# Other PSUM banks for the second FFN chunk, and a new order of the first FFN steps on three engines

## The reference, cut to what matters

```python
h = rmsnorm(x, ffn_norm)
g = jnp.einsum('bsd,df->bsf', h, w_gate)      # 1024 x 2816
u = jnp.einsum('bsd,df->bsf', h, w_up)        # 1024 x 2816
x = x + jnp.einsum('bsf,fd->bsd', jax.nn.silu(g) * u, w_down)   # 2816 x 1024
return rmsnorm(x, final_norm)
```

## Time and profile before

| | |
|---|---|
| median of 3 runs | 301.69 us (301.49, 301.69, 302.96) |
| profiled execution, its own time | 301.57 us |
| its span in the trace | 299.8 us |
| mean granted TensorE clock | 0.982 |
| PE busy | 287.1 us, 96% of the span |
| DVE busy | 265.1 us, 88% |
| ACT busy | 189.7 us, 63% |
| DMA, HBM read | 55.72 MB, 190 GB/s over the span |

### The profile page before, as it was taken

One profiled execution on the slowest core, in us unless ns is written; L12 is line 12 of the kernel. 1 busy time (PEld: TensorE's weight loads), 2 busy tenths in 40 slices (PEclk: granted clock), 3 DMA queues, 4 the chain that ended last, 5 costly groups with the idle time before them and its releaser, 6 DMA issues.

```text
span 299.8 us, 4081 instructions
## 1 busy us (share of the span) xinstructions
PE 287.1 (96%) x1396; PEld 234.5 (78%) x1396; DVE 265.1 (88%) x413; ACT 189.7 (63%) x312; POOL 21.2 (7%) x27
## 2 busy tenths in 40 slices
PE   8999999999999999599999999999999999999990
PEld 4788888878888888478888888888888888888870
DVE  3888999998998679877999999999999999999794
ACT  4878569664986459645656565757566666565424
POOL 0011000000123307000000000000000000000040
PEclk9999999999999999869999999999999999999997
DMA  7999617798878737747667676697967766240003
GB/s 255 386 420 360 202 37 236 226 280 246 233 215 215 272 103 267 224 141 263 204 206 229 201 229 217 215 289 233 285 202 215 237 212 226 88 159 19 2 0 140
DMA packets 29797, 62.87 MB, mean 210 GB/s; under 512 B 3792, under 2 KB 17104, under 8 KB 28368
## 3 DMA queue, kind: packets, MB, share of 16 engines
q1 hardware_dynamic: 27616, 61.03, 62.4%
q10 hardware_dynamic: 2160, 1.59, 1.7%
HBM read 55.72 MB, written 1.11 MB: 190 GB/s over the span
## 4 chain that ended last, share of the span: by engine, by line
PE 85%; ACT 5%; DVE 4%; issue 3%; DMA 2%; SPq 0%; POOL 0%; POOLq 0%; ACTq 0%
PE bank L556 27%; PE bank L557 27%; PE bank L558 27%; PE bank L633 2%; DMA room<-in_first 2%; PE bank L583 1%; ACT w_hi L873 1%; DVE qkT_lo L1299 1%; ACT x_hi L888 1%; PE bank L606 1%; ACT probs L898 1%; DVE xs L1430 0%; PE bank L609 0%; DVE xs L1436 0%; ACT L1069 0%
## 5 line engine op out<-in xcount | busy, mean ns | idle before, releaser
L556 PE MATMUL bank<-w_hi,x_hi 128*128 128x512 f32 x230 | 92.3, 401 | 3.6 <-ACT room L1018 3.2
L558 PE MATMUL bank<-w_hi,x_lo 128*128 128x512 f32 x230 | 90.6, 394 | 0.0
L557 PE MATMUL bank<-w_lo,x_hi 128*128 128x512 f32 x230 | 90.5, 394 | 0.0
L556 PEld LDWEIGHTS bank<-w_hi,x_hi 128*128 128x128 f32 x230 | 43.8, 191 | 14.2 <-ACT room L1018 3.7
L558 PEld LDWEIGHTS bank<-w_hi,x_lo 128*128 128x128 f32 x230 | 43.7, 190 | 9.3
L557 PEld LDWEIGHTS bank<-w_lo,x_hi 128*128 128x128 f32 x230 | 43.9, 191 | 8.8
L873 ACT ACTIVATE w_hi<-raw 128x1024 fp32r<-128x1024 f32 x33 | 33.7, 1050 | 10.0 <-issue 9.6
L1141 DVE TENSOR_TENSOR w_lo<-raw,w_hi 128x1024 fp32r<-128x1024 f32 x32 | 38.3, 1212 | 1.2 <-ACT w_hi L873 1.1
L1299 DVE TENSOR_TENSOR w_lo<-raw,w_hi 128x1024 fp32r<-128x1024 f32 x30 | 35.7, 1214 | 0.4
L1017 ACT ACTIVATE rope_b<-bank,rstd 128x256 f32<-128x256 f32 x22 | 10.4, 475 | 40.0 <-PE bank L558 40.0
L1006 ACT ACTIVATE w_hi<-raw 128x1024 fp32r<-128x1024 f32 x29 | 29.4, 1054 | 0.0
(11 more groups left out here) (143 smaller groups left out, 465.6 us busy)
## 6 DMA issues: line engine op xcount, KB each, us to landing
raw<-in_weights SPq DMA_DIRECT2D x74, 512.0 KB, 5.5
room<-in_weights SPq DMA_DIRECT2D x10, 1024.0 KB, 5.6
room<-room SPq DMA_DIRECT2D x76, 64.0 KB, 2.4
room<-in_first SPq DMA_DIRECT2D x3, 384.0 KB, 5.0
room<-in_first SPq DMA_DIRECT2D x1, 1024.0 KB, 8.5
xs<-in_x SPq DMA_DIRECT2D x2, 512.0 KB, 9.8
rot<-turned_sums SPq DMA_DIRECT2D x8, 128.0 KB, 4.9
room<-room ACTq DMA_DIRECT2D x12, 64.0 KB, 2.8
```

The costliest lines, as they stand in the source:

```text
L556: pe.matmul(dst, a_hi, w1, start=first, stop=False)
L557: pe.matmul(dst, a_hi, w2, start=False, stop=False)
L558: return pe.matmul(dst, a_lo, w1, start=False, stop=last)
```

## The change

- The second chunk's gate and up go to banks 6 and 7 (`GU_FIRST`, `gate_up_bank`), so PE no longer waits for evacuations before it. The wait for "all four evacuations" before `down_second(0)`, which stood in front of its third product, stands in front of its first; chunk 2, which uses bank 4 alone, waits for the first evacuation where it waited for the third.
- On ACT, the third pair of chunk 1 comes ahead of the squares of the residual; both evacuations of chunk 0 come ahead of its first forms; and in step 1 the operands of chunk 0's hidden part come ahead of the splits for chunk 2.
- On DVE, products and turns of chunk 0 come ahead of its down sums and first forms, and sums and rests of its hidden part come right behind them, ahead of the splits for chunk 2.
- POOL's and SP's lists are unchanged.

```diff
--- before.py
+++ after.py
@@ -88,6 +88,7 @@
             5: (H_E, RAW_P), 6: (H_F, RAW_R), 7: (H_G, RAW_Q)}
 PRODUCT_BANK = {1: 0, 2: 1, 5: 2, 3: 3, 7: 6, 6: 7, 4: 5}
 GU_BANK = 4
+GU_FIRST = (4, 5), (6, 7)
 
 
 COLUMNS = (0, 0), (0, 1), (1, 0), (1, 1), (0, 2), (1, 2)
@@ -304,6 +305,9 @@
         down_lo = o_lo[:].rearrange("p a s -> p (a s)").rearrange("p (b n) -> p b n", n=NB)
         more_hi = qkT_hi[:].rearrange("p a h s -> p (a h s)").rearrange("p (b n) -> p b n", n=NB)
         more_lo = qkT_lo[:].rearrange("p a h s -> p (a h s)").rearrange("p (b n) -> p b n", n=NB)
+
+        def gate_up_bank(c, s):
+            return bank[GU_FIRST[c][s] if c < 2 else GU_BANK]
 
         def gate_up_at(c, k, n):
 
@@ -721,7 +725,7 @@
 
                 cols = slice(s * P, (s + 1) * P)
                 w1, w2 = gate_up_at(c, k, 1)
-                dst = bank[GU_BANK + s if c < 2 else GU_BANK]
+                dst = gate_up_bank(c, s)
                 ins = three_products(dst[:], x_hi[:, k, cols], x_lo[:, k, cols], w1[:, 0, :], w2[:, 0, :],
                                      k == 0, k == KT - 1)
                 if k == KT - 1:
@@ -752,9 +756,9 @@
             def down_second(c, order=(7, 6, 4)):
 
                 pe.wait_ge(down_lo_ready, 2 * c + 2)
+                if c == 0:
+                    pe.wait_ge(evacuated, 4)
                 for n in order:
-                    if c == 0 and n == 4:
-                        pe.wait_ge(evacuated, 4)
                     at = PRODUCTS[n][1] - FORMS_B[0]
                     ins = product(c, n, down_hi[:, at, :], down_lo[:, at, :])
                 ins.then_inc(down_done, 1)
@@ -830,15 +834,13 @@
                     first_chunk(k, s)
             for h in range(2):
                 for s in range(SH):
-                    if h == 0:
-                        pe.wait_ge(evacuated, s + 1)
                     gate_up_half(1, s, h)
             pe.wait_ge(res_done, 8)
             down_first(0)
 
             def step(c):
 
-                pe.wait_ge(evacuated, 2 * c if c > 2 else 3)
+                pe.wait_ge(evacuated, 2 * c if c > 2 else 1)
                 for h in range(2):
                     gate_up_half(c, 0, h)
                 down_second(c - 2)
@@ -1013,7 +1015,7 @@
                 act.wait_ge(gu_done, 2 * c + s + 1)
                 if c:
                     act.wait_ge(hid_ready, SH * (c - 1) + s + 1)
-                src = bank[GU_BANK + s if c < 2 else GU_BANK]
+                src = gate_up_bank(c, s)
                 act.activation(silu[:, s, :], src[:, 0:FC], ACT.Silu, scale=rstd[:, 6 + s:7 + s])
                 act.activation(up[:, s, :], src[:, FC:2 * FC], ACT.Copy,
                                scale=rstd[:, 6 + s:7 + s]).then_inc(evacuated, 1)
@@ -1064,18 +1066,21 @@
             gate_up_hi(1, 1)
             item(("ffnturn", 2))
             item(("ffnturn", 3))
+            gate_up_hi(1, 2)
             residual_squares(1)
 
             act.activation(warm_out[:, 1:2], warm[:, 0:1], ACT.Silu)
-            gate_up_hi(1, 2)
             gate_up_hi(1, 3)
-            down_first_hi(0)
             evacuate(0, 0)
             evacuate(0, 1)
+            down_first_hi(0)
             act.dma_start(gain_out, final_norm.partition_broadcast(P)).then_inc(in_gout, 16)
 
             def step(c):
 
+                if c == 1:
+                    hidden_hi(0)
+                    hidden_sums_hi(0)
                 if c < NCH - 1:
                     gate_up_hi(c + 1, 0)
                     gate_up_hi(c + 1, 1)
@@ -1086,9 +1091,8 @@
                     down_second_hi(c - 2)
                 if c < NCH - 1:
                     gate_up_hi(c + 1, 2)
-                hidden_hi(c - 1)
-                if c == 1:
-                    hidden_sums_hi(0)
+                if c > 1:
+                    hidden_hi(c - 1)
                 evacuate(c, 0)
                 if c > 1:
                     hidden_sums_hi(c - 1)
@@ -1377,11 +1381,13 @@
             gate_up_lo(1, 1)
             gate_up_lo(1, 2)
             gate_up_lo(1, 3)
-            down_sums(0)
-            down_first_lo(0)
             for s in range(SH):
                 multiply(0, s)
                 turn_squares(0, s)
+            down_sums(0)
+            down_first_lo(0)
+            hidden_sums(0)
+            hidden_lo(0)
 
             def step(c):
 
@@ -1393,10 +1399,10 @@
                     last_down_lo(1)
                 if c > 1:
                     down_second_lo(c - 2)
-                hidden_sums(c - 1)
                 if c > 1:
+                    hidden_sums(c - 1)
                     down_sums(c - 1)
-                hidden_lo(c - 1)
+                    hidden_lo(c - 1)
                 if c < NCH - 1:
                     gate_up_lo(c + 1, 2)
                 else:
```

## The result

| | before | after |
|---|---|---|
| median | 302.60 us (20 runs, 300.34 to 304.07) | 303.24 us (20 runs, 302.12 to 306.61) |
| ratio | 1 | 1.0045, 95% interval 1.0023 to 1.0066 |
| profiled execution, span | 301.57, 299.8 us | 303.22, 301.4 us |
| granted clock, mean | 0.982 | 0.979 |

The change makes the kernel slower by a few tenths of a percent: 0.45% by the ratio in the table, which is estimated from all runs and not only from the medians; the quotient of the two medians is 1.0021. Forecast was 300.1 us, 0.5% faster, with a range of 298.4 to 302.3; the measured 303.24 us lies outside it. The runs of each kernel spread over about 4 us, more than the first three had shown.

What follows compares the result with a forecast made beforehand. PE, busy 96% of the span, was taken as the bound. Filling its hole gains 6.1 us, less 2.9 for a new wait and 1.7 for the clock: 1.5 us, from 301.57 to 300.1 us, range 298.4 to 302.3.

Steps and rivals of the forecast that it cites:

- the new wait before `down_second(0)`: PE reaches it at 142.23, the second forms are ready at 145.1: a wait of 2.9 us, bounds 1.9 to 4.0.
- The sum: Whole kernel: 6.1 (hole filled) - 2.9 (new wait) - 1.7 (clock again) = 1.5 us gained.
- The hole is filled, 6.1 us: Ahead of chunk 1's first matmul on PE: 3.4 us of wait and 2.7 of slow clock go.
- Squares of the residual at no cost, evacuations and turns done at 125.2, sums at 125.2: ACT and DVE around chunk 0's evacuations: moving the squares costs nothing; place DMAs and sums start at 125.2.
- The squares land 4.1 us after the issue: Chunk 0's place DMAs, issued at 125.2, land at 129.3; about 130.9 by the ring-order rule, costing 0.3 us.
- rival C: Chunk 3's second pair lands at 143.5: wait 5.7 us, clock 2.7, kernel 2.3 us slower, 303.9; chance 0.12.
- No wait at `down_first(0)`, 1 us to spare: Chunk 0's last hidden rest is ready at 133.1; PE comes for it at 134.07.
- The second load of chunk 3 lands at 140.7, a wait of 2.9 us: Load of chunk 3's second weight pair: issued at 135.7, taking 5.0 us; PE then waits at `down_second(0)`.
- The clock costs 1.7 us: PE's clock falls again with the wait at `down_second(0)`; 1.7 us taken between nothing and 2.7.
- DVE is done with the first forms' rest at 153.1: At `down_first(1)`: DVE finishes at 153.1, PE arrives at 154.3, so PE does not wait.
- PE keeps its 15.6 us a step from there on: Steps after `down_first(1)`: PE holds 15.6 us a step against DVE's 14.8 to 15.3.

Runs made afterwards that it cites:

- e5: The changed kernel with the 512 KB DMA of the final norm's gain issued in step 4 instead of among chunk 0's place DMAs; 1.0039 of before.
- e12: The changed kernel measured again with nothing altered, beside other versions; 1.0032 of before.
- e3: The changed kernel with 18 matmuls of zeros into free bank 5 ahead of PE's wait for the second forms; 1.0073 of before.
- e10: e6 with the DMA of the final norm's gain issued in step 4; 0.9977 of before.
- e6: The changed kernel with the first two splits of chunk 2 back ahead of chunk 0's hidden operands on ACT and DVE; 0.9908 of before.
- e20: The same code as e6, measured again; 0.9937 of before.
- e17: The kernel before with only the DMA of the final norm's gain moved to step 4; 1.0008 of before.
- e1: PE's part of the change only (chunk 1 in banks 6 and 7), ACT and DVE in the order of before; 0.9967 of before.

## Why the prediction was wrong

The step that failed is the new wait before `down_second(0)`. The sum had 2.9 us for it, and by the starts of matmuls it took 4.9 (4.6 of idle time, the rest is slow starts). Behind it stand two DMA times that were put too low: the squares of chunk 0, 6.7 us from the first issue where the sum had 4.1, and the load of chunk 3's second pair, 6.2 us where it had 5.0. Smaller parts are 0.4 us at `down_first(0)`, which stood at nothing, and 2.3 instead of 1.7 us for the clock: 0.4 + 2.0 + 0.6 is the 3.0 us between the 1.5 gained of the forecast and the 1.5 lost. Part by part:

- *The hole is filled, 6.1 us.* Right: no wait ahead of chunk 1, and the clock was 1.0 until 145.3.
- *Squares of the residual at no cost, evacuations and turns done at 125.2, sums at 125.2.* Right within 0.2 us (125.17 for the place DMAs).
- *The squares land 4.1 us after the issue.* Wrong: 6.7 us, at 131.90. In e5, without the gain's DMA among them, it was 5.0 us. So 1.7 of the 2.6 us are that DMA; the other 0.9 stay, and would have cost nothing, since DVE came for them at 130.5. I had moved that DMA with the first forms and not counted it against the squares; rival C names it, but ahead of chunk 3's loads, and it had landed at 126.3 + 4.2 = 130.5, long before they went out. The late squares made all behind them 1.3 us later.
- *No wait at `down_first(0)`, 1 us to spare.* 0.3 us of wait, by the same 1.3 us.
- *The second load of chunk 3 lands at 140.7, a wait of 2.9 us.* The mechanism was right, and the size failed: the load went out 1.3 us late and took 6.2 us, at the bound (6.1) and not at the 5.0 that I took. It landed at 143.28, and the wait was 4.6 us. In e12 it took 5.2 us and the wait was 3.6: the late issue comes back, a part of the slow landing belongs to the one execution.
- *The clock costs 1.7 us.* At half clock were 4.58 us of work, 2.3 us. But e3 shows that this term was not additive: DVE would have held PE but for 0.7 us.
- *DVE is done with the first forms' rest at 153.1.* It was 156.6: 2.4 us by the later start of the second forms' rest (145.74 instead of 143.3), and 1.05 by the wait for chunk 1's squares at 148.54, for which the walk had nothing. PE had been there at 155.81 in before. So 0.8 us of the loss stand by DVE alone, whatever the clock does.
- *The sum.* 6.1 - 0.4 (wait and restart at 134.5) - 4.9 (wait and restart at 147.5) - 2.3 = -1.5 us, by starts of matmuls, instead of +1.5. This is near the milder half of rival C, to which I had given 0.06, and at its edge: C's landing was 143.5, but its wait 5.7 and its clock 2.7.
- *PE keeps its 15.6 us a step from there on.* True in the first profile of the changed kernel (rest 144.1 against 144.0), not in general: in e12 it is 1.1 us longer, in e5 1.3, in e10 5.4. DVE's 14.8 us in 15.6 leave less than 1 us for a late DMA, and I had used that as if nothing disturbed it.

What stays open: which arrangement of loads makes the squares land late. The same code gave 9.5 us of idle time in one profile and 5.9 in another (e6, e20). Why the squares of the early orders land about 1 us later than those of before even without the gain's DMA isn't shown either. And with one profile for each, a ratio can't be explained to 0.2%.

## What to carry to other kernels

When a wait on the bounding engine is removed, walk the engine behind it (here DVE) to the next two places, with every DMA landing at the late end of its range, before any gain is booked. Work that waits for a DMA belonged, in this kernel, behind work that was ready and fed the next load: two splits ahead of the squares' operands turned 0.3 to 0.5% slower into 0.6 to 0.9% faster. A DMA that is moved along with a neighbour counts as a change of its own. Where the engine behind the bounding one is 95% busy in the steady state, as DVE is here, a faster start can be given back later, so the start's profile isn't the result.

## What the runs showed that I had not expected

- One wait, two prices of the clock. PE waited 3.23 us ahead of chunk 1 in the profile of before, and 3.28 in that of e17, which is the same code there. In before the clock fell inside the wait and 5.5 us of work were slow; in e17 it fell 1.2 us after it, for 3.41 us:

```profile
126.79:127.95 1.16, 1.16 (x5) 0.98 (x6) 1.16 (x1) 1.16 (x3) 0.00 (x0) 1.00 0.49 198
127.95:131.36 3.41, 3.41 (x10) 2.64 (x9) 3.34 (x7) 2.36 (x3) 0.00 (x0) 0.50 0.02 4
```

  The start was 0.9 us shorter, and 1.1 is what the 2.1 us less of slow work are worth. So a part of the run-to-run spread can be the clock's. Of the runs of before beside e1, the 8 with a mean clock of 0.99 or more have a median of 300.9 us and the 4 with 0.984 or less 302.8; the runs of before beside e5 and e12, on other chips, show no such link.
- The length of a wait alone doesn't say whether the clock falls. It fell with waits of 3.23 (before) and 2.26 us (e1), and stayed at 1.0 through and behind one of 2.85 (e5). The prediction's choice of 1.7 us, between nothing and 2.7, had no row that could settle it.
- A 512 KB DMA on ACT's queue made the last of four 64 KB DMAs on SP's queue take 4.5 to 5.2 us, in seven profiles, where five without it have 3.1 to 3.7.
- The same 64 KB DMAs took 5.8 us between 150 and 270 when POOL issued them, against 2.6 from SP.
